# A Fourier stage that sums even and odd tokens apart: half the columns of the token tables, the halves joined on VectorE

## The reference, cut to what matters

```python
def fourier_mix(u):
    B, L = u.shape[:2]
    ug = u.astype(jnp.float32).reshape(B, L, FOURIER_GROUPS, FOURIER_GROUP_DIM)
    y = jnp.fft.fft2(ug, axes=(1, 3), norm='ortho').real
    return y.reshape(B, L, FOURIER_WIDTH).astype(u.dtype)
```

## Time and profile before

| | us |
|---|---|
| median of 3 runs | 3031.27 |
| lowest and highest run | 3030.39 and 3034.31 |
| span of the profiled execution | 3033.5 |
| Fourier stage in it, first token matmul to first matmul of the next block | 308.68 to 349.52 |

### The profile page before, as it was taken

How to read it: one execution, slowest core, us unless ns; L and a number is a source line. 1 busy time by engine, 2 the same in 40 slices (tenths; PEclk the granted TensorE clock), 3 DMA queues, 4 the chain that set the end, 5 groups by cost and what they waited for, 6 DMA issues and landing times.

```text
span 3033.5 us, 32637 instructions
## 1 busy us (share of the span) xinstructions
PE 2688.2 (89%) x11875; PEld 2053.1 (68%) x11875; DVE 1827.2 (60%) x2790; ACT 1256.7 (41%) x1754; POOL 151.8 (5%) x186
## 2 busy tenths in 40 slices
PE   5689989899888599999499888999989997899998
PEld 1468566666676487878386656888868675678886
DVE  5743167677676798999637666444453666544444
ACT  5423235444433377777433254322233315432222
POOL 0011000000000011111001100000000110000000
PEclk9899999999999799999689989999998997999999
DMA  8457324443441599999223331222222334222222
GB/s 318 145 153 210 91 62 125 123 109 92 147 166 71 189 370 368 365 357 352 96 91 115 104 114 61 91 94 92 97 65 79 115 97 127 68 84 97 84 96 76
DMA packets 237689, 436.41 MB, mean 144 GB/s; under 512 B 71272, under 2 KB 94048, under 8 KB 237567
## 3 DMA queue, kind: packets, MB, share of 16 engines
q1 hardware_dynamic: 220335, 391.79, 39.7%
q0 software_dynamic: 17232, 43.02, 4.2%
HBM read 399.91 MB, written 50.56 MB: 148 GB/s over the span
## 4 chain that ended last, share of the span: by engine, by line
PE 49%; DVE 16%; DMA 5%; ACT 5%; issue 4%; DVEq 0%; SPq 0%; POOL 0%; ACTq 0%; POOLq 0%
PE BKP L774 36%; DVE WL L2636 2%; DMA W<-in_w_expert_gu_dram 2%; ACT WH L1723 1%; DVE G L2244 1%; DMA W<-in_w_expert_down_dram 1%; PE BKP L1009 1%; DMA G<-in_w_expert_gu_dram 1%; DVE hL L2636 1%; PE BKP L1197 1%; PE BKP L1200 1%; PE BKP L1199 1%; DVE WL L1939 1%; PE SCP L1278 1%; PE SCP L1237 1%
## 5 line engine op out<-in xcount | busy, mean ns | idle before, releaser
L1939 DVE TENSOR_TENSOR WL<-W,WH 128x2048 fp32r<-128x2048 f32 x130 | 297.9, 2292 | 480.0 <-ACT WH L1343 478.6
L1343 ACT ACTIVATE WH<-W 128x2048 fp32r<-128x2048 f32 x130 | 248.7, 1914 | 608.5 <-PE BKP L774 545.5
L774 PE MATMUL BKP<-hH,WH 128*128 128x512 f32 x896 | 356.4, 398 | 8.0 <-DVE hL L2381 5.9
L774 PE MATMUL BKP<-hH,WL 128*128 128x512 f32 x896 | 352.1, 393 | 0.0
L774 PE MATMUL BKP<-hL,WH 128*128 128x512 f32 x896 | 352.0, 393 | 0.0
L774 PE MATMUL BKP<-WH,aH 128*128 128x512 f32 (+1 forms) x544 | 215.9, 397 | 22.3 <-DVE aL L2616 10.6
L774 PE MATMUL BKP<-WL,aH 128*128 128x512 f32 (+1 forms) x544 | 212.2, 390 | 0.0
L774 PE MATMUL BKP<-WH,aL 128*128 128x512 f32 (+1 forms) x544 | 212.2, 390 | 0.0
L774 PE MATMUL BKP<-WH,hH 128*128 128x512 f32 (+3 forms) x512 | 201.3, 393 | 6.9 <-ACT Z L1394 2.7
L774 PEld LDWEIGHTS BKP<-hH,WH 128*128 128x128 f32 x896 | 170.8, 191 | 49.3 <-issue 10.4
L774 PEld LDWEIGHTS BKP<-hL,WH 128*128 128x128 f32 x896 | 170.2, 190 | 36.5
(11 more groups left out here) (490 smaller groups left out, 5679.9 us busy)
## 6 DMA issues: line engine op xcount, KB each, us to landing
W<-in_w_expert_gu_dram SPq DMA_DIRECT2D x46, 1024.0 KB, 7.6
G<-in_w_expert_gu_dram SPq DMA_DIRECT2D x46, 1024.0 KB, 7.7
W<-in_w_in_dram SPq DMA_DIRECT2D x42, 1024.0 KB, 5.4
W<-in_w_up_dram SPq DMA_DIRECT2D x32, 1024.0 KB, 5.2
W<-in_w_down_dram SPq DMA_DIRECT2D x32, 1024.0 KB, 5.1
W<-in_w_expert_down_dram SPq DMA_DIRECT2D x24, 1024.0 KB, 7.1
G<-in_w_expert_down_dram SPq DMA_DIRECT2D x22, 1024.0 KB, 6.6
X<-in_w_in_dram SPq DMA_DIRECT2D x16, 1024.0 KB, 6.8
```

Source lines behind the costliest of these rows:

```text
L774: mm = pe.matmul(BK[j][:, 0:cols], lt, rh, start=start and a == 0, stop=stop and a == len(q) - 1, skip_group_check=True)
L1343: act.activation(WH[s][:], W[s][:] if raw is None else raw, ACT.Copy).then_inc(sems["w_hi"], 1)
L1939: v.tensor_tensor(WL[s][:], W[s][:] if raw is None else raw, WH[s][:].bitcast(F32), ALU.subtract).then_inc(sems["w_lo"], 1)
```

## The change

The tokens of the Fourier input are dealt out by parity. In the "T" form the stationary operand of column tile j now takes every second column of hH or hL, so that tiles 0 and 2 hold even tokens and tiles 1 and 3 odd ones. One table of 1024 KB takes the place of two: for each token, 256 cosines and 256 sines, for the output frequencies below 256. The token sums of a group are four matmuls instead of eight: tiles 0 and 2 into one PSUM bank (E), tiles 1 and 3 into the next (O). DVE copies O to a row of Z, then writes E + O and E - O into F. F stays a single buffer, so the adds of group g wait for the feature sums of group g - 1 (`fo_b`). E and O have two places in PSUM, SCP and the first two banks of BKP, and PE makes the token sums of groups 0 and 1 ahead of everything, and those of groups 2 and 3 after the feature sums of groups 0 and 1. PE waits for all four banks once before the stage. ACT keeps only its copy of TPP.

```diff
+        FOU = [SC[:, :], BKP[:, 0:1024]]
...
-            load(BV[:, 0:4, :], t["k_dftc"].rearrange("(k p) s -> p k s", p=P), "fou_landed")
-            load(BV[:, 4:8, :], t["k_dfts"].rearrange("(k p) s -> p k s", p=P), "fou_landed")
+            load(BV[:, 0:4, :], t["k_dft"].rearrange("(k p) s -> p k s", p=P), "fou_landed")
...
-                                q.append((ap[:, k0 + k, j * P:(j + 1) * P], wp[s][:, k, 0:n]))
+                                q.append((ap[:, k0 + k, cols_at(j)], wp[s][:, k, 0:n]))
...
-            blk(h, "T")
-
-            pe.wait_ge(sems["fou_landed"], T.next("fou_landed", 48))
+            halved = lambda j: slice(j // 2 * 256 + j % 2, j // 2 * 256 + 256, 2)
+            unit(h, 0, "T", UN, True, False, cols_at=halved)
+            unit(h, 4, "T", UN, False, True, cols_at=halved)
+
+            pe.wait_ge(sems["fou_landed"], T.next("fou_landed", 32))
             pe.wait_ge(sems["fou_in"], T.next("fou_in"))
-            for g in range(4):
-                for part in range(2):
-                    for k in range(4):
-                        mm = pe.matmul(SC[:, part * 512:(part + 1) * 512], TM[:, k, g * P:(g + 1) * P],
-                                       BV[:, part * 4 + k, :], start=k == 0, stop=k == 3)
+            for b in BANKS:
+                pe.wait_ge(sems[b], T.at(b))
+            def token_sums(g):
+                for j in (0, 2, 1, 3):
+                    mm = pe.matmul(FOU[g % 2][:, j % 2 * 512:(j % 2 + 1) * 512], TM[:, j, g * P:(g + 1) * P], BV[:, j, :],
+                                   start=j < 2, stop=j >= 2, skip_group_check=True)
                 mm.then_inc(sems["fo_a"], 1)
+            def feature_sums(g):
                 pe.wait_ge(sems["fo_cp"], T.next("fo_cp"))
                 if g:
                     pe.wait_ge(sems["fo_o"], T.next("fo_o"))
                 for part in range(2):
                     mm = pe.matmul(TP[:, 0:512], DG[:, part * P:(part + 1) * P], F[:, part, :],
                                    start=part == 0, stop=part == 1)
                 mm.then_inc(sems["fo_b"], 1)
+            token_sums(0)
+            token_sums(1)
+            for g in range(4):
+                feature_sums(g)
+                if g < 2:
+                    token_sums(g + 2)
...
             for g in range(4):
-                act.wait_ge(sems["fo_a"], T.next("fo_a"))
-                act.activation(flat(F[:]), SC[:], ACT.Copy).then_inc(sems["fo_cp"], 1)
                 act.wait_ge(sems["fo_b"], T.next("fo_b"))
                 act.activation(ST[0][:, g, :], TP[:, 0:512], ACT.Copy).then_inc(sems["fo_o"], 1)
...
-            for _ in range(4):
+            def fourier(g):
+                odd = Z[:, 2 + g % 2, 0:512]
+                parts = lambda ap: ap.rearrange("p (a k) -> p a k", a=2)
+                v.wait_ge(sems["fo_a"], T.next("fo_a"))
+                link(v.tensor_copy(odd, FOU[g % 2][:, 512:1024]))
+                if g:
+                    v.wait_ge(sems["fo_b"], T.at("fo_b", g))
+                v.tensor_tensor(F[:, :, 0:256], parts(FOU[g % 2][:, 0:512]), parts(odd), ALU.add)
+                v.tensor_tensor(F[:, :, 256:512], parts(FOU[g % 2][:, 0:512]), parts(odd), ALU.subtract).then_inc(
+                    sems["fo_cp"], 1)
+            for _ in range(3):
                 blk()
+            for g in range(4):
+                fourier(g)
+            blk()
```

More of the change, by code:

```diff
@@ L751, in _, with unit @@
             h, cx, aa = (hH[:], hL[:]), (cH, cL), (aH[:], aL[:])
-            def unit(act, k0, form, n, start, stop, nj=4, ready=None, each=None):
+            def unit(act, k0, form, n, start, stop, nj=4, ready=None, each=None, cols_at=lambda j: slice(j * P, (j + 1) * P)):
                 s = slot[0]
@@ L2901, in tables @@
     al = 2 * np.pi * ((tok[:, None] * tok[None, :]) % S) / S
+    halved = np.concatenate([j // 2 * 256 + j % 2 + 2 * np.arange(P) for j in range(NT)])
     g = np.arange(P)
@@ L2920, in tables @@
         "k_rets": tiles(np.sin(ang2)),
-        "k_dftc": (np.cos(al) / np.sqrt(S)).astype(f),
-        "k_dfts": (np.sin(al) / np.sqrt(S)).astype(f),
+        "k_dft": (np.concatenate([np.cos(al[halved, 0:S // 2]), np.sin(al[halved, 0:S // 2])], 1) / np.sqrt(S)).astype(f),
         "k_dftg": (np.concatenate([np.cos(ag), -np.sin(ag)], 1) / np.sqrt(P)).astype(f),
```

## The result

The changed kernel takes 3009.1 us, the median of 4 runs (3006.77 to 3015.92), against 3032.06 us for the kernel before (4 runs, 3030.39 to 3034.31). The ratio is 0.9929, with a 95% interval of 0.9915 to 0.9943. That is 21.5 us less (17.3 to 25.8). The forecast was 17.6 us less, 3013.7 us, with a range of 3010 to 3022. The profiled execution took 3008.59 us with a span of 3006.8, so 1.8 us lie around the span.

The account below looks back on a forecast made before the run. The stage was taken as a chain of PE and ACT alone, PE idling 1.37 us per group for ACT's copy. Matmuls (13.8 us) and idle time (3.9) gave 17.7, 17.6 by layout: 3013.7 us, range 3010 to 3022.

Parts of the forecast that it names:

- The sum: Fourier stage: its end moves from 349.52 to 331.94, 17.6 us earlier, so the kernel's median becomes 3013.7 us.
- The one hole: Before the last group's feature sums: PE idles 1.55 us for DVE's adds, in place of four idle times of 1.37.
- The strided loads: Block before the stage, 96 loads of every second column: a load may grow 39 ns before pacing; taken as nothing.
- The rivals that doubled or quadrupled the load: Block before the stage: loads of 376 ns give 3028.0 us (chance 0.04), loads of 752 ns 3064 us (0.03).
- The term 96 x (load - 0.227): Block before the stage: added time when loads exceed the 0.227 us matmul distance; 14.3 us if doubled, 50.4 if quadrupled.
- DVE's rows: DVE operations taking every second element cost 1220 against 1218 ns; used to price the strided weight loads at nothing.
- The clock: Fourier stage: rival that the clock falls to the 1.2 GHz level, 20.6 us more, 3034 us; chance 0.01.
- DVE is not hidden: Fourier stage: rival that PE waits for DVE's whole chain in each group, 9.1 us, giving 3021.2 us; chance 0.05.
- The shift arrives: Behind the stage: later work keeps its distances, so 17.6 us reach the end; rival of absorption, 3031 us, chance 0.04.
- The sign that the time behind the stage stays at 2684 us: From the stage's end to the span's end: the time should be unchanged, 2684 us.

Follow-up runs that it names:

- e6: The kernel before with only the Fourier input's block loading every second column and both tables' rows permuted to match, against the kernel before: 0.9996.
- e7: The kernel before with only the Fourier input's block loading every fourth column and both tables' rows permuted to match, against the kernel before: 0.9997.
- e2: The changed kernel without the look-ahead, each group's token sums directly followed by its feature sums, against the kernel before: 3026.03 us, 0.9981.
- e9: The kernel before with ACT's copy into F made twice, one after the other, lengthening PE's hole in each group, against the kernel before: 3039.98 us, 1.0028.
- the second: The changed kernel again with no edit, against the kernel before: 3011.1 us, 0.9937.
- e5: The kernel before against itself, with no edit: 3030.34 us, 0.9991.
- all four comparisons: Against the kernel before: the changed kernel twice (0.9929, 0.9937), and twice with its last feature sums behind the next block's first column tile (0.9920, 0.9919).

## Why the prediction held

**The sum.** The stage was to become 331.94 - 308.68 = 23.26 us and is 23.24 and 23.25. The parts hold one by one. 32 matmul instructions at 0.43 us are gone. DVE's three take 0.72, 0.61 and 0.69 us, and the adds on two pieces of 256 cost what a piece of 512 does. The first group's copy was to start 3.76 us after the first matmul, and starts after 3.71. The last feature sums were to start after 20.59 us, and start after 20.57. The one hole was to be 1.55 us by steps. By the same count it is 1.61 (the last matmul before it starts at 332.02); the 1.45 of the bracket goes by a modelled end. A little luck is in the last hundredths: the matmuls stand 0.429 us apart and not 0.43, and the last group's first add starts 0.70 us behind its matmul and not 0.63, and the two cancel. The end, 2.67 us from them to the next block, is the same. What follows keeps its distances: the weights' rounding starts 0.12 us behind the block's first matmul, and the next waits 9.23 us for PE, both as before.

**The strided loads, mis-sized.** The step said that a load may grow by 39 ns before it sets the pace, and took nothing. The loads grew by 5 ns and the matmuls moved apart by 6.7 ns, 0.64 us in the block (e6 shows it by itself). The rivals that doubled or quadrupled the load fell with 193 ns. The way in which they were priced failed too. The term 96 x (load - 0.227) takes a load to begin only when the last has ended. For e7's load of 310 ns it would give 8.0 us, and the block there was 0.8 us longer, with loads that overlap. What 376 or 752 ns would cost no run shows. DVE's rows, by which I chose the lower end, gave nearly the right size, but by luck, since they say nothing of PE's loads.

**The clock, not asked rightly.** The forecast gave a fall of the clock 0.01 and argued that the stage had four holes and now has one. For the kernel as changed that held, 1.00 throughout. But the cover was costed only by its length: "DVE is not hidden" was priced at 3021.2 us, 7.5 us above the forecast. The kernel in which it is not hidden (e2) ran at 3026 us. Its holes were as costed, 2.27 us each by steps, but they also brought the clock down in the stage and for part of the next block. e9 shows that the holes alone do it.

**The shift arrives.** No stretch behind the stage took the gain back. The excess over the steps, with 21.5 us measured in the first comparison and 19.1 in the second against 17.0, is 4.5 and 2.1 us; two identical programs gave 2.7 (e5). The sign that the time behind the stage stays at 2684 us did not come true: it was 2670.1 and 2674.0. But the same program as before had 2677.0 (e5), and the rest goes with the granted clock, which differs from profile to profile of one program. So I take the excess for that variation, which is argued and not shown. Whether some 2 or 3 us of it belong to the change stays open: all four comparisons of versions with halved tables and look-ahead gave more than the steps (17.0, 17.0, 19.6 and 19.6 us by the traces; 21.5, 19.1, 24.3 and 24.6 measured), and no stretch was found that holds it. The range was too narrow at its lower end for this: it allowed 3.7 us below the forecast, and the median came 4.6 below.

## What to carry to other kernels

Cost a hand-over between engines by layout, step by step from rows of the same shapes; it was right here to 0.02 us in 23. Put independent matmuls into a hole not only for its length: here lengthening the holes to over 2 us cost 1.6 times the added length (e2: 12.3 us for 7.5) to twice (e9: 8.5 for 4.2) through the clock, where holes of 1.4 us cost only themselves. When one stage is changed in a long kernel, compare that stage in the traces, and compare the whole program with itself once, since single executions of the same program can differ by nearly as much as the change: in e5's comparison the kernel before took from 3023.39 to 3039.65 us.

## What the runs showed of the hardware

- The granted clock averaged 0.82 and 0.64 over parts of a stage whose PE idle times were 2.1 us (e2), and 0.76 and 0.72 where they were 2.2 us between 8.6 us of matmuls (e9). It stayed below 1.00 for part of the block behind (0.84, 0.85, 0.81), though PE was busy there without a break.
- A weight load of 128 columns in fp32r took 188 ns contiguous, 193 ns with a step of 8 bytes, and 310 ns with a step of 16 bytes, while matmuls stood 0.2266, 0.2333 and 0.2350 us apart. The loads of 310 ns are shown overlapping.
- An fp32 matmul of 512 columns ran as two instructions, each 0.43 us, and DVE's add of two 256-element pieces from PSUM took 0.69 us, as one of 512 does.
